# Norm offsets behind the first MLP chunk's low halves, last group's low halves before an addition, two weight splits before dt's chain

## What is computed

```python
for i in range(2):
    if i == 0:                      # bidirectional Mamba-2 mixer
        mix = ssd_mixer(x, in_proj, conv_w, conv_b, dt_bias, a_log, d_skip, norm_w, out_proj)
    else:                           # pooling mixer: band averages, four 512x512 products, bias, scale
        mix = pool_mixer(x, pool_w, pool_b, pool_scale)
    x = layer_norm(alpha * x + mix, ln_mix_g[i], ln_mix_b[i])
    x = layer_norm(alpha * x + square(relu(x @ w1[i])) @ w2[i], ln_ffn_g[i], ln_ffn_b[i])
```

## Time and profile before

| | |
|---|---|
| median of 3 runs | 2204.94 us (2203.26 to 2205.19) |
| the profiled execution | 2205.52 us |
| its span in the trace | 2203.8 us |
| TensorE busy | 2163.3 us, 98% |
| VectorE busy | 1439.6 us, 65% |
| ScalarE busy | 1109.6 us, 50% |
| GpSimd busy | 234.0 us, 11% |
| DMA | 443.96 MB, mean 201 GB/s |

### The profile page before, as it was taken

How to read it: one execution, slowest core, us unless ns; L and a number is a source line. 1 busy time by engine, 2 the same in 40 slices (tenths; PEclk the granted TensorE clock), 3 DMA queues, 4 the chain that set the end, 5 groups by cost and what they waited for, 6 DMA issues and landing times.

```text
span 2203.8 us, 31261 instructions
## 1 busy us (share of the span) xinstructions
PE 2163.3 (98%) x10626; PEld 1817.0 (82%) x10626; DVE 1439.6 (65%) x1778; ACT 1109.6 (50%) x1549; POOL 234.0 (11%) x172
## 2 busy tenths in 40 slices
PE   9999999999999999999999999989999999999997
PEld 7788888888887778888888888867888888888886
DVE  6787867858768855555565655696565655555656
ACT  5677747757665544444353443446343443443433
POOL 0213322303310500000000000033000000000001
PEclk9999999999999999999999999999999999999999
DMA  8969896988956665555555555446555555555553
GB/s 272 252 202 237 237 278 180 238 230 227 239 183 221 203 212 184 182 200 176 205 190 190 195 185 180 168 152 227 191 191 190 200 181 187 194 180 200 190 191 115
DMA packets 246963, 443.96 MB, mean 201 GB/s; under 512 B 14048, under 2 KB 49040, under 8 KB 245216
## 3 DMA queue, kind: packets, MB, share of 16 engines
q1 hardware_dynamic: 206608, 397.52, 53.8%
q0 software_dynamic: 35664, 28.66, 7.6%
q10 hardware_dynamic: 4608, 16.78, 2.0%
HBM read 440.68 MB, written 2.23 MB: 201 GB/s over the span
## 4 chain that ended last, share of the span: by engine, by line
PE 85%; DVE 7%; DMA 3%; ACT 2%; issue 2%; DVEq 0%; ACTq 0%; SPq 0%
PE acc L357 13%; PE acc L359 13%; PE acc L358 13%; PE acc L608 9%; PE acc L615 5%; PE tb L608 5%; PE sbk L608 5%; DVE wlo L1101 3%; PE sbk L359 3%; PE sbk L357 3%; PE tb L357 3%; PE tb L359 3%; PE tb L358 3%; PE sbk L358 3%; PE sbk L615 2%; PE tb L615 2%
## 5 line engine op out<-in xcount | busy, mean ns | idle before, releaser
L718 ACT CAST whi<-raw 128x1024 fp32r<-128x1024 f32 x746 | 774.8, 1054 | 672.2 <-DMA raw<-in_w 269.8
L1101 DVE TENSOR_TENSOR wlo<-raw,whi 128x1024 fp32r<-128x1024 f32 x746 | 920.4, 1271 | 195.9 <-ACT whi L718 191.4
L357 PE MATMUL acc<-whi,xT 128*128 128x512 f32 x800 | 322.0, 402 | 12.7 <-DVE wlo L1101 10.9
L359 PE MATMUL acc<-wlo,xT 128*128 128x512 f32 x800 | 312.8, 391 | 0.0
L358 PE MATMUL acc<-whi,xT 128*128 128x512 f32 x800 | 312.2, 390 | 0.0
L357 PE MATMUL acc<-whi,hTl 128*128 128x512 f32 x768 | 304.6, 397 | 6.0 <-DVE hTl L1121 3.3
L358 PE MATMUL acc<-whi,hTh 128*128 128x512 f32 x768 | 299.8, 390 | 0.0
L359 PE MATMUL acc<-wlo,hTh 128*128 128x512 f32 x768 | 299.8, 390 | 0.0
L608 PE MATMUL acc<-xT,whi 128*128 128x512 f32 x896 | 224.0, 392 | 0.0
L357 PEld LDWEIGHTS acc<-whi,xT 128*128 128x128 f32 x800 | 150.7, 188 | 49.0 <-issue 9.0
L608 PEld LDWEIGHTS acc<-xT,whi 128*128 128x128 f32 x896 | 162.0, 189 | 29.6
(11 more groups left out here) (207 smaller groups left out, 2675.0 us busy)
## 6 DMA issues: line engine op xcount, KB each, us to landing
raw<-in_w SPq DMA_DIRECT2D x512, 512.0 KB, 4.7
raw<-in_in_proj SPq DMA_DIRECT2D x162, 512.0 KB, 5.4
raw<-in_out_proj SPq DMA_DIRECT2D x64, 512.0 KB, 7.4
spare<-in_masks ACTq DMA_DIRECT2D x16, 512.0 KB, 7.4
spare<-f_scratch POOLq DMA_DIRECT2D x32, 256.0 KB, 15.4
area_d<-in_masks ACTq DMA_DIRECT2D x8, 512.0 KB, 5.9
area_d<-f_scratch POOLq DMA_DIRECT2D x16, 256.0 KB, 6.9
area_c<-in_masks ACTq DMA_DIRECT2D x8, 512.0 KB, 7.2
```

The source lines that it names most:

```text
L357: pe.matmul(dst, lhs[1][:, kt, rows(t)], hi, start=first and i == 0, stop=False)
L359: mm = pe.matmul(dst, lhs[0][:, kt, rows(t)], lo, start=False, stop=end)
L718: act.copy(whi[:, s.slot(RING)], raw[:, r]).then_inc(hi_ready, 1)
L1101: dve.tensor_tensor(wlo[:, slot], raw[:, r], whi[:, slot].bitcast(F32), ALU.subtract).then_inc(lo_ready, 1)
```

## The change

Three edits. In `narrow_group(1)` the splits of pieces s+8 and s+9 are moved ahead of `dt_steps(0)` on both ScalarE and VectorE. At the end of the mixer, `gy_low(Pos(7))` is moved ahead of the two additions of group `Q_D3+3`, behind the splits of `S_D3+10` and `S_D3+11`. In both layers the eight offset additions on GpSimd wait no longer for the transposed x (`tr_lo`) but for the last low halves of h in the first chunk (`h_lo[1]`).

```diff
@@ ScalarE, narrow_group
                         if k == 1:
+                            split_hi(s + 8)
+                            split_hi(s + 9)
                             dt_steps(0)
...
-                blocks(s, 2, 4, after, done=4)
+                blocks(s, 2, 4, after, done=6 if k == 1 else 4)
@@ VectorE, narrow_group
                     if n == 1 and k == 1:
+                        split_lo(s + 8)
+                        split_lo(s + 9)
                         dve.wait_ge(acc_free[Q_DT % 2][0], 2)
                         dt_steps(0)
-                blocks(s, 2, 4, after, done=4)
+                blocks(s, 2, 4, after, done=6 if k == 1 else 4)
@@ VectorE, end of the mixer
             down(Pos(Q_D3 + 2), Pos(S_D3 + 4), 2, none, 2, done=2)
-            down(Pos(Q_D3 + 3), Pos(S_D3 + 6), 3, none, 2)
+            for i in range(2):
+                split_lo(Pos(S_D3 + 10 + i))
             gy_low(Pos(7))
+            down(Pos(Q_D3 + 3), Pos(S_D3 + 6), 3, none, 2, done=2)
@@ GpSimd
-            def offsets(i, first):
+            def offsets(i):
 
                 gain_q3(i)
-                pool.wait_ge(tr_lo, first + 8)
+                pool.wait_ge(h_lo[1], i + 2)
...
-            offsets(0, 0)
+            offsets(0)
...
-            offsets(2, 16)
+            offsets(2)
```

## The result

The changed kernel takes 2213.21 us (median of 5 runs, 2212.63 to 2214.89) where the kernel before takes 2204.94 (5 runs beside it, 2202.34 to 2206.63): 8.3 us or 0.39% slower, ratio 1.0039 with a 95% interval of 1.0028 to 1.0050. The forecast was 2210 us, with a range of 2201 to 2217. The profiled execution took 2213.21 us with a span of 2211.5, which is 7.7 us above the span before.

The account below looks back on a forecast made before the run. TensorE, busy 98% of the span, bounds the kernel, so edits act only through its waits. Terms 0.35 + 0 + 0.8 + 2.4 + 0 + 1.2 give +4.8 on 2205.52 us; with the median 0.6 lower, 2210 us, range 2201 to 2217.

Parts of the forecast that it names:

- its own case: Whole kernel: the forecast without its rivals, 2206 us (no clock drop) to 2213 us (three more drops); chance 0.46.
- dt's chain: First edit: TensorE's wait moves from s+8 to s+10 and ScalarE's copies, transposes start at 68.3; +0.35 us.
- Low halves: Mixer's end: waits of 2.35 and 0.38 us become one of 3.1; 0 us, low end -2.5 if loads come sooner.
- the 1.2 us put down for the clock: First two edits' merged waits: one clock drop of 1.6 us, likelier than not, entered as 1.2 us.
- Won in layer 0: Layer 0's first chunk up to `tb`: without GpSimd's work there, it runs as layer 1's; -5.47 us.
- Cost in layer 0: `tb`, layer 0: s+25 and s+26 wait under GpSimd's operations (2.9, 3.2 us); +0.8 net of the gain, +2.4 for the clock.
- three waits: `tb` in layer 0: profile sign of strict alternation, against the forecast's two waits, near 790 and 794.
- Layer 1, 0: Layer 1's first chunk: no three operations there, so the later additions stay hidden; 0 us, up to +3.
- Strict alternation: Layer 0's `tb`: operations hold s+26 to the end and get in before s+27; 5.9 us later, 2216 us; chance 0.22.
- VectorE keeps its lead: Layer 0's `tb`: splits run back to back while GpSimd waits, nothing given back; -5.1 us, 2200 us; chance 0.09.
- mild slowing: Layer 0's `tb`: splits take 2.3 us each, TensorE waits 1.1 us; 2201 us; chance 0.13.
- Layer 1 did not wait: Answers the rival that layer 1 waits for s+24 or s+28: +1 to +4 on the forecast, 2213 us; chance 0.10.

Follow-up runs that it names:

- dt_only: The kernel before with only the splits of s+8 and s+9 moved ahead of `dt_steps(0)`: 2203.82 us, ratio 0.9998.
- offsets_only: The kernel before with only the offset additions' wait changed from `tr_lo` to `h_lo[1]`, in both layers: 2213.22 us, ratio 1.0039.
- all_late: The kernel before with layer 0's gains load, pooling scale and bias loads and three bias operations moved into its second to fourth chunk: 2200.58 us, ratio 0.9984.
- low_all_late: all_late with `gy_low(Pos(7))` also moved ahead of the additions at the end of the mixer: 2196.8 us, ratio 0.9972.

## Why the prediction came out as it did

**Direction and place were right, the size came out low.** 2210 was forecast and 2213.2 measured, +4.8 us against +8.3. That is inside the range, and just above the 2213 that the prediction gave as the most of its own case. The slowdown comes from the three operations of GpSimd's that fall on the splits behind the offset additions in layer 0, with a slow clock behind them, as forecast.

- *dt's chain, +0.35.* In the profile +0.67 with the two waits moved as described, but 0.3 of that was there before the edit's place, where the convolution began 0.3 us later. By itself the edit makes no difference that the runs show. The step is right within what can be measured.
- *Low halves, 0.* In the changed kernel it went as told: the fourth group at 697.30, one wait in place of two, then seven slow matmuls. With these TensorE was 1.90 us late at the last transposes where it had been 0.82 late at the mixer's last; the 1.2 us put down for the clock covers that. What I took as fixed is not: the load took 11.33 us in one execution and 8.42 in another, and there the 2.5 us that I kept as the low end were won. Nor do show that a wait of 2.35 us alone leaves the clock up: their stretch ends at 688.00, before TensorE goes on at 688.14. The clock did stay up in that execution, but in dt_only, offsets_only and all_late it fell behind the same wait.
- *Won in layer 0, -5.47.* Between the two profiled executions the term was right: TensorE wanted s+24 at 790.0, within 0.1 us of the 788.2 of the prediction plus the 1.9 us that it was late by then. But the kernel before was at its dear end there. Three others with the same code show 1.7 to 2.5 us above the floor of 67.8, and the time moved by 2.9 when the operations were taken away. It was too large by about half, as a statement on the median.
- *Cost in layer 0, +0.8 net and +2.4 for the clock, 3.2 together.* Measured 4.75 us in the profile, and offsets_only has 6.3 in C. The mechanism is the one given, but which splits are held is not. I let s+24 slip ahead of the first operation because it would begin 0.4 us earlier; it did begin 0.39 us earlier and was held 6.05 us all the same. s+25 took the 4.67, s+26 passed, and s+27, which was to be ready in time, was held for 5.57. So there were three waits and not two. They put TensorE's starts off by 6.9 us where the two of the forecast had 6.1, and some 15 matmuls ran at half clock where 2.4 us stands for 12. That the waits came this near in sum owes something to luck: with s+24 held for 2.85 us, s+25 cost 1.91 where I had 2.9, s+26 nothing where I had 3.2, and s+27 1.14.
- *Layer 1, 0.* Right: x ready after 10.0 us of additions, splits undisturbed, no wait at `tb` or `sbk`.
- *Not in the sum at all*: 1.2 us in the pooling stage, which no edit touches, with the clock at 0.72 where it was 1.00.

**The rivals.** Strict alternation (2216) had two parts. Its second came true: L1699 got in before s+27, TensorE waited a third time, and three waits are what the prediction itself named as the sign of this rival. Its first did not: s+26 passed between two operations. The run lies about half way between the forecast and this rival. That VectorE keeps its lead is refuted by the 6.05 us, and mild slowing by all three long splits. Layer 1 did not wait.

What stays open: why a split gets its turn beside the offset additions (2.0 us each in the earlier trace rows) and beside the third set of quarters (1.9), and not beside the first (6.45 us, though of the same shape); and what makes the clock fall in one execution and not in another behind the same wait, at the end of the mixer and in the pooling stage.

## What to carry to other kernels

Moving work off an engine's busy place moves all that is queued behind it too: the additions themselves were hidden, and what cost 8 us were three operations written after them whose result GpSimd first uses some 640 us later (at 1447 in the changed kernel). Give such work its own wait in a gap of the engine that it hinders, here a count of finished splits, and do the same with loads that stand beside the loads of weights. And read a stretch in several executions before its difference becomes a term of a sum: here one profile said 5.5 us where the median moved by 2.9.

## What the runs showed of the hardware

- A VectorE subtraction with both inputs in SBUF (1.2 us alone) is held until a 128x2048 operation of GpSimd's on two tensors ends, even when its record begins 0.39 us earlier: 6.05 us beside a start at 787.27 and an end at 791.84. The Trainium skill ("SBUF — State Buffer", SBUF: two separate sides) says that whichever starts first gets the shared ports for its whole instruction. The exclusion agrees with the trace for L1694 and L1699, less for L1696 (tensor times a constant), whose record ends 0.64 us after the split beside it did; that the record which begins first wins does not agree.
- Four operations of 128x512 back to back held one split through all of them (6.45 us), while quarters of a tensor times a constant let splits through at 1.6 us, and later quarters of a tensor plus a tensor at 1.9.
- VectorE's operations with one input in PSUM were not held: the low halves of h, which take 0.68 us alone, took 0.68 and 0.69 us inside L1688 (751.95 to 756.96) in the kernel before:

```profile
752.40 0.68 DVE L1121 TENSOR_TENSOR hTl<-tb,hTh 128x512 fp32r<-128x512 f32 x1
755.30 0.69 DVE L1121 TENSOR_TENSOR hTl<-tb,hTh 128x512 fp32r<-128x512 f32 x1 [2.22 <-ACT hTh L1004]
```

- Two 1 MB loads issued by GpSimd beside 512 KB loads issued by SyncE went with 8.4 to 11.3 us for the latter at the end of the mixer; with nothing beside them such loads took 4.5 us in the same place (median in low_all_late).
- Behind one and the same wait of 2.35 us the granted clock stayed at 1.00 in three executions and fell in three others (0.57 over 4 us in dt_only), and M is about 1 us longer in those (52.8 to 53.0 against 51.8 to 52.0).
